# Where the sums of the modulation stand in the expert stages of a diffusion trunk on one core

## The chip, the cores and the metric

One NeuronCore of a Trainium2 chip runs the kernel. The metric is the device time of one execution in microseconds, as the median of several runs. The engines are TensorE (PE: matrix products, with its weight loads shown apart as PEld), VectorE (DVE), ScalarE (ACT), GpSimd (POOL) and SyncE (SP), which issues the loads.

## The reference, cut to what matters

One step of a hybrid trunk with four layers, on 128 context tokens and 256 latent tokens at a width of 1024, in float32. A layer has a token mixer (gated MLP, Mamba-2 SSD, HGRN2, gated MLP) and then a grouped top-2 mixture of 16 experts. Both sub-layers are modulated by vectors that come from the conditioning, one set for the context and one for the latent tokens:

```python
def modulation(cond, w_mod, b_mod):
    m = jax.nn.silu(cond) @ w_mod + b_mod          # (1024) @ (1024, 6*1024)
    return jnp.split(m[:, None, :], 6, axis=-1)    # shift, scale, gate, twice
...
gate, up = jnp.split(jnp.einsum('ld,edf->lef', xs, w_gu), 2, axis=-1)
hid = jax.nn.silu(gate) * up * cw[..., None]
return jnp.einsum('lef,efd->ld', hid, w_down)
```

The modulation of a layer needs nothing of the tokens, so it can be computed at any time before its layer.

## The kernel before, in words

Everything runs on one core with the order of each engine's work written out by hand; semaphores tie the engines together. All large weights come in chunks of 1 MB through one ring of eight slots in SBUF, in the fixed order of a plan; the loads are issued by SP (L393), each as soon as the chunk that held its slot before has been used.

**The modulation.** A layer has six groups of 1024 modulation values, and a group has four weight chunks (`MOD_GROUP` is 4). The DVE multiplies the rows of a chunk by the conditioning and adds them up over the chunks in `macc`, 128 partitions by 1024 columns for each of the two sets (L1961, L1964; four instructions a chunk). What is left is a sum over the 128 partitions. That is `mod_sum` on TensorE (L1690): for each of the 16 blocks of 128 columns of `macc`, the block is the stationary operand and one column of ones the moving one, and the product is one column of PSUM bank 7. Each float32 product appears in the trace as two passes, so a group is 32 passes of one column. `mod_take` on the DVE (L1972) then reads the 16 columns, adds the bias and writes `mods`. Only after it may the DVE start the next group's `macc`.

**The expert stage.** `experts(l)` on TensorE routes and gathers the tokens and then runs 24 steps (6 windows of 128 tokens, 4 experts each). Step `s` is `gate_up(s)`: eight products of 128x128 by 128x512 (L1877, two passes each, 16 in all) from weight chunks A and B into PSUM bank `s % 2`. After the sixth product stand the two transpositions of the step before (`hidden_over(s - 1)`, L1867, bank 2). Then comes `down(s - 1)`: four products of 128x512 (L1892, 8 passes) from chunk D. ACT computes the SiLU of the gate half (`sg`, L1518) and copies the transposed hidden values (`hidt`, L1493); the DVE forms `hid` (L2182). In layers 0, 1 and 2, 16 of the 24 steps (0, 1, 3, 4, 6, 7, ... 21, 22) also bring one chunk of the next layer's modulation (four groups), which the DVE adds into `macc` after that step's `hid`. A group is complete after steps 4, 10, 16 and 22. TensorE runs its `mod_sum` one step later, after `down` of that step, all 16 products in a row (L1903). The DVE takes the sums two steps after the group's last chunk, behind `hid`. Layer 3 has no layer behind it and no modulation in its expert stage.

Of the kernel before, what the change touches and what calls it, by code (L numbers as in the profile page):

```python
# [55 lines left out]
MOD_GROUP = MODC // 6  # L56
# [5 lines left out]
STEPS = NW * EG  # L62
# [12 lines left out]
def moe_mods(l):  # L75

    n = MODC - 2 * MOD_GROUP
    return {j * STEPS // n: j for j in range(n)} if l + 1 < DEPTH else {}
# [90 lines left out]
def trunk(nc, A, O):  # L169
# [13 lines left out]
    with ctx:  # L183
# [13 lines left out]
        def fixed(name, shape, dt=F32):  # L197
            t = at(name, shape, dt, place[0])
            place[0] += -(-4 * int(np.prod(shape[1:])) // 32) * 32
            return t  # L200
# [16 lines left out]
        mods = fixed("mods", [P, 2, 48, 2])  # L217
# [1179 lines left out]
        def chunk_in(eng, c):  # L1397
            eng.wait_ge(raw_in[slot_of[c]], 16 * fill_of[c])
# [215 lines left out]
        def _(pe):  # L1614
            release = {}

            def claim(b, name, value):

                if b in release:
                    pe.wait_ge(*release[b])  # L1620
                release[b] = (S[name], value)
# [61 lines left out]
            def mod_sum(group, columns=range(2 * KD)):  # L1683

                if 0 in columns:
                    pe.wait_ge(S["mac_step"], 16 * (group_of_mac(group) + 1))
                    claim(7, "mod_read", group + 1)
                for c in columns:
                    j, v = divmod(c, 2)
                    ins = pe.matmul(ps[:, 7, c:c + 1], macc[:, v, j * P:(j + 1) * P], ones[:, 0:1], start=True, stop=True)  # L1690
                if 2 * KD - 1 in columns:
                    ins.then_inc(S["mod_summed"], 1)
# [104 lines left out]
            def experts(l):  # L1797
                n0, q, mods = STEPS * l, 2 * l + 1, moe_mods(l)
# [57 lines left out]
                def whole(what, s, k):  # L1856
                    c = places[l, what][s]
                    return ring[:, slot_of[c], :].rearrange("p (k n) -> p k n", k=k)

                def hidden_over(s):  # L1860
                    pe.wait_ge(S["hid_ready"], n0 + s + 1)
                    if s == 0:
                        claim(2, "hidt_ready", n0 + STEPS)
                    elif s >= 2:
                        pe.wait_ge(S["hidt_ready"], n0 + s - 1)
                    for i in range(2):
                        ins = pe.transpose(ps[:, 2, (s % 2) * DE + i * P:(s % 2) * DE + (i + 1) * P], hid[:, s % 2, i * P:(i + 1) * P], ident[:, :])  # L1867
                    ins.then_inc(S["hidt_done"], 1)

                def gate_up(s):  # L1870
                    w, e = divmod(s, EG)
                    claim(s % 2, "hid_ready", n0 + s + 1)
                    for k in range(KD):
                        what = "AB"[k // 4]
                        if k % 4 == 0:
                            chunk_in(pe, places[l, what][s])
                        ins = pe.matmul(ps[:, s % 2, :], xg[:, w, k, :], whole(what, s, 4)[:, k % 4, :], start=(k == 0), stop=(k == KD - 1))  # L1877
                        if k % 4 == 3:
                            ins.then_inc(S["moe_used"], 1)
                        if s and k == 5:  # L1880
                            hidden_over(s - 1)

                def down(s):
                    w, e = divmod(s, EG)
                    chunk_in(pe, places[l, "D"][s])
                    pe.wait_ge(S["hidt_ready"], n0 + s + 1)
                    if e == 0:
                        for h in range(2):
                            claim(OUT_BANKS[w % 2][h], "olo_ready", 2 * (NW * l + w) + h + 1)
                    for k in range(2):  # L1890
                        for h in range(2):
                            ins = pe.matmul(ps[:, OUT_BANKS[w % 2][h], :], hidt[:, s % 2, k, :], whole("D", s, 2)[:, k, 512 * h:512 * h + 512],  # L1892
                                            start=(e == 0 and k == 0), stop=(e == EG - 1 and k == 1))
                    ins.then_inc(S["moe_used"], 1)
# [3 lines left out]
                for s in range(STEPS):  # L1898
                    gate_up(s)
                    if s:  # L1900
                        down(s - 1)
                        if s - 1 in mods and mods[s - 1] % MOD_GROUP == MOD_GROUP - 1:
                            mod_sum(6 * (l + 1) + 1 + mods[s - 1] // MOD_GROUP)  # L1903
                hidden_over(STEPS - 1)
                down(STEPS - 1)
# [22 lines left out]
            for l in range(DEPTH):  # L1928
                if l % 3 == 0:
                    gmlp(l)  # L1930
                elif l % 3 == 1:
                    pe_ssd(pe, l, claim, release, full, by_token, out_tiles, product, row_blocks, full_block)
                else:
                    pe_hgrn(pe, l, claim, release, full, by_token, out_tiles, mod_sum, product, row_blocks, full_block)
                variance(2 * l, 6 * l + 6 if l + 1 < DEPTH else None)
                if l + 1 < DEPTH:
                    mod_sum(6 * l + 6, range(6, 2 * KD))
                experts(l)
                variance(2 * l + 1)
# [365 lines left out]
```

## Time and profile before

| | |
|---|---|
| median of 3 runs | 2907.91 us (2905.69, 2907.91, 2911.71) |
| profiled execution: span from the first to the last instruction | 2919.7 us |
| its time beside the span | the profile gives none |
| mean granted TensorE clock over the span | 0.913 |
| TensorE busy | 2612.8 us, 89% |
| VectorE busy | 1430.2 us, 49% |
| GpSimd, ScalarE busy | 797.6 us, 752.2 us |
| DMA | 524.41 MB, mean 180 GB/s |

All times are microseconds unless marked ns. The granted clock is a share of full speed: 1.00 is 2.4 GHz, 0.50 is 1.2 GHz, and a value between them is the mean over a stretch that has both. Matmuls overlap at their ends, so what a pass costs in a stream is read from the starts of neighbouring lines, not from its own duration. The profile is of one execution that is not among the three timed ones.

### The profile page before, as it was taken

To read this page: it belongs to the slowest core of one execution; us is meant where nothing else is said; L and a number is where in the kernel's file an instruction comes from. 1 tells how busy PE (TensorE), PEld (TensorE's weight loads), DVE (VectorE), ACT (ScalarE), POOL (GpSimd) and SP (SyncE) were. 2 spreads that over 40 slices of the span, in tenths; PEclk is the share of its full clock that TensorE was granted. 3 is DMA by queue.
4 is the path that set the end of the run, shared out by engine and by line. 5 is a ranking of instruction groups with operands and counts; after the bars stand their busy time and mean duration, and the time that the engine had idled before them with its cause. 6 is when DMAs were issued, how large, how long until landed. Compare 5 with 4: busy or idle time off the path is not lost.

```text
span 2919.7 us, 30216 instructions
## 1 busy us (share of the span) xinstructions
PE 2612.8 (89%) x11960; PEld 1918.1 (66%) x11960; DVE 1430.2 (49%) x1955; ACT 752.2 (26%) x1263; POOL 797.6 (27%) x429
## 2 busy tenths in 40 slices
PE   5779899998898998899998877789999899989997
PEld 3778864445896787744458866676444699864444
DVE  6456553334645676633336389974333415650013
ACT  1132130002454451300013344432001334230111
POOL 3355400001363344000014478830000247500000
PEclk8789889998699998899999878898999899979999
DMA  7443639893241216388944411054989143528881
GB/s 265 168 124 101 193 143 334 321 360 110 76 137 37 73 58 180 137 326 316 362 162 138 143 48 37 24 183 150 332 324 348 51 135 101 149 99 300 301 297 41
DMA packets 291851, 524.41 MB, mean 180 GB/s; under 512 B 9472, under 2 KB 141056, under 8 KB 291328
## 3 DMA queue, kind: packets, MB, share of 16 engines
q1 hardware_dynamic: 288256, 519.33, 51.4%
q10 hardware_dynamic: 3456, 3.15, 0.3%
q8 instruction: 96, 1.57, 0.2%
q14 instruction: 43, 0.35, 0.0%
HBM read 517.73 MB, written 4.72 MB: 179 GB/s over the span
## 4 chain that ended last, share of the span: by engine, by line
PE 75%; DVE 12%; ACT 4%; DMA 3%; issue 3%; POOL 2%; SPq 0%; ACTq 0%; DVEq 0%
PE ps L1877 23%; PE ps L1892 11%; PE ps L1625 6%; PE ps L1626 6%; PE ps L1627 6%; PE ps L1690 3%; DVE macc L1964 2%; POOL wlo L1557 2%; DVE uw L1318 2%; PE ps L1648 1%; PE ps L1816 1%; PE ps L1650 1%; PE ps L1649 1%; PE ps L1840 1%; PE ps L1841 1%
## 5 line engine op out<-in xcount | busy, mean ns | idle before, releaser
L1557 POOL TENSOR_TENSOR wlo<-ring,whi 128x1024 fp32r<-128x1024 f32 x202 | 533.6, 2657 | 1514.3 <-ACT whi L1424 1514.3
L1877 PE MATMUL ps<-ring,xg 128*128 128x512 f32 x1536 | 708.0, 606 | 0.0
L1877 PEld LDWEIGHTS ps<-ring,xg 128*128 128x128 f32 x1536 | 290.5, 194 | 329.6 <-issue 329.2
L1964 DVE SCALAR_TENSOR_TENSOR macc<-ring,cond_s,macc 128x1024 f32<-128x1024 f32 x322 | 438.9, 1424 | 10.6 <-DMA ring<-w_mod 10.6
L2182 DVE SCALAR_TENSOR_TENSOR hid<-ps,cws,sg 128x256 f32<-128x256 f32 x96 | 46.4, 484 | 674.6 <-ACT sg L1518 674.6
L1892 PE MATMUL ps<-ring,hidt 128*128 128x512 f32 x768 | 349.9, 599 | 2.3 <-ACT hidt L1493 2.3
L1625 PE MATMUL ps<-hh,whi 128*128 128x384 f32 x832 | 303.4, 365 | 27.3 <-POOL wlo L1557 21.0
L1626 PE MATMUL ps<-hl,whi 128*128 128x384 f32 x832 | 291.0, 350 | 0.0
L1627 PE MATMUL ps<-hh,wlo 128*128 128x384 f32 x832 | 290.9, 350 | 0.0
L1424 ACT ACTIVATE whi<-ring 128x1024 fp32r<-128x1024 f32 x202 | 207.2, 1055 | 307.4 <-DMA ring<-gmlp_w_out 115.2
L1892 PEld LDWEIGHTS ps<-ring,hidt 128*128 128x128 f32 x768 | 147.4, 193 | 187.4 <-issue 187.4
L1493 ACT ACTIVATE hidt<-ps 128x256 f32<-128x256 f32 x96 | 37.0, 385 | 753.9 <-PE ps L1867 753.9
L1625 PEld LDWEIGHTS ps<-hh,whi 128*128 128x128 f32 x832 | 166.7, 200 | 34.7 <-POOL wlo L1557 23.1
L1648 PE MATMUL ps<-whi,hh 128*128 128x256 f32 x432 | 132.7, 307 | 50.7 <-POOL wlo L1557 46.8
L1626 PEld LDWEIGHTS ps<-hl,whi 128*128 128x128 f32 x832 | 166.9, 201 | 0.5 <-issue 0.5
L1627 PEld LDWEIGHTS ps<-hh,wlo 128*128 128x128 f32 x832 | 165.9, 199 | 0.0
L1649 PE MATMUL ps<-whi,hl 128*128 128x256 f32 x432 | 130.6, 302 | 0.0
L1650 PE MATMUL ps<-wlo,hh 128*128 128x256 f32 x432 | 130.3, 302 | 0.0
L1648 PEld LDWEIGHTS ps<-whi,hh 128*128 128x128 f32 x432 | 91.9, 213 | 52.3 <-POOL wlo L1557 48.0
L1690 PEld LDWEIGHTS ps<-ones,macc 128*128 128x128 f32 x736 | 100.8, 219 | 11.1 <-issue 8.7
L1625 PE MATMUL ps<-gsh,whi 128*128 128x384 f32 x256 | 91.7, 358 | 17.7 <-POOL wlo L1557 17.1
L1690 PE MATMUL ps<-ones,macc 128*128 128x1 f32 x736 | 98.5, 267 | 1.0 <-DVE macc L1964 1.0
(361 smaller groups left out, 4112.3 us busy)
## 6 DMA issues: line engine op xcount, KB each, us to landing
ring<-moe_w_gu SPq DMA_DIRECT2D x192, 1024.0 KB, 7.5
ring<-w_mod SPq DMA_DIRECT2D x96, 1024.0 KB, 8.2
ring<-moe_w_down SPq DMA_DIRECT2D x96, 1024.0 KB, 5.1
ring<-gmlp_w_in SPq DMA_DIRECT2D x32, 1024.0 KB, 5.7
ring<-ssd_w_in SPq DMA_DIRECT2D x21, 1024.0 KB, 5.3
ring<-hgrn_w_in SPq DMA_DIRECT2D x20, 1024.0 KB, 5.2
ring<-gmlp_w_out SPq DMA_DIRECT2D x16, 1024.0 KB, 5.7
ring<-ssd_w_out SPq DMA_DIRECT2D x8, 1024.0 KB, 6.0
```

The costliest lines, as they stand in the source:

```text
L1424: act.activation(split_sub(whi, s0), raw_sub(s0), ACT.Copy).then_inc(S["hi_ready"], 1)
L1557: pool.tensor_tensor(split_sub(wlo, s0), raw_sub(s0), split_sub(whi, s0).bitcast(F32), ALU.subtract).then_inc(S["lo_ready"], 1)
L1625: pe.matmul(out, lhi, rhi, start=first, stop=False)
L1626: pe.matmul(out, lhi, rlo, start=False, stop=False)
L1627: return pe.matmul(out, llo, rhi, start=False, stop=last)
L1648: pe.matmul(outs[t], hh[:, k, tk], pair(whi, k), start=(k == 0), stop=False)
L1649: pe.matmul(outs[t], hl[:, k, tk], pair(whi, k), start=False, stop=False)
L1650: ins = pe.matmul(outs[t], hh[:, k, tk], pair(wlo, k), start=False, stop=(k == KD - 1))
L1690: ins = pe.matmul(ps[:, 7, c:c + 1], macc[:, v, j * P:(j + 1) * P], ones[:, 0:1], start=True, stop=True)
L1877: ins = pe.matmul(ps[:, s % 2, :], xg[:, w, k, :], whole(what, s, 4)[:, k % 4, :], start=(k == 0), stop=(k == KD - 1))
L1892: ins = pe.matmul(ps[:, OUT_BANKS[w % 2][h], :], hidt[:, s % 2, k, :], whole("D", s, 2)[:, k, 512 * h:512 * h + 512], start=(e == 0 and k ...
L1964: ins = dve.scalar_tensor_tensor(out=macc[:, v, :], in0=w[:, k, :], scalar=by, in1=macc[:, v, :], op0=ALU.mult, op1=ALU.add)
```

## The change

Where a group was complete after step `s - 2`, `gate_up(s)` now issues two of the group's 16 single-column products after each of its own eight products. Where there is no such step, after step 22 (`s` would be 24), the row stays where it was, after `down(22)` in step 23. So in each of the layers 0, 1 and 2 the sums of steps 4, 10 and 16 move from the end of steps 5, 11 and 17 into steps 6, 12 and 18. `mod_sum` itself is as before: its waits stand before the first column, its signal after the last.

```diff
                 def gate_up(s):
                     w, e = divmod(s, EG)
+                    group = 6 * (l + 1) + 1 + mods[s - 2] // MOD_GROUP if s - 2 in mods and mods[s - 2] % MOD_GROUP == MOD_GROUP - 1 else None
                     claim(s % 2, "hid_ready", n0 + s + 1)
                     for k in range(KD):
                         what = "AB"[k // 4]
...
                         ins = pe.matmul(ps[:, s % 2, :], xg[:, w, k, :], whole(what, s, 4)[:, k % 4, :], start=(k == 0), stop=(k == KD - 1))
                         if k % 4 == 3:
                             ins.then_inc(S["moe_used"], 1)
+                        if group is not None:
+                            mod_sum(group, range(2 * k, 2 * k + 2))
                         if s and k == 5:
                             hidden_over(s - 1)
...
                     gate_up(s)
                     if s:
                         down(s - 1)
-                        if s - 1 in mods and mods[s - 1] % MOD_GROUP == MOD_GROUP - 1:
+                        if s == STEPS - 1 and mods.get(s - 1, 0) % MOD_GROUP == MOD_GROUP - 1:
                             mod_sum(6 * (l + 1) + 1 + mods[s - 1] // MOD_GROUP)
```

## Rows read from the trace of the kernel before

**Rows 1.** The page, part 1: busy time, share of the span, instructions.

```profile
PE 2612.8 (89%) x11960; PEld 1918.1 (66%) x11960; DVE 1430.2 (49%) x1955; ACT 752.2 (26%) x1263; POOL 797.6 (27%) x429
```

**Rows 2.** The page, part 4: the chain that ended last, by engine and line.

```profile
PE 75%; DVE 12%; ACT 4%; DMA 3%; issue 3%; POOL 2%; SPq 0%; ACTq 0%; DVEq 0%
PE ps L1877 23%; PE ps L1892 11%; PE ps L1625 6%; PE ps L1626 6%; PE ps L1627 6%; PE ps L1690 3%; DVE macc L1964 2%; POOL wlo L1557 2%; DVE uw L1318 2%; PE ps L1648 1%; PE ps L1816 1%; PE ps L1650 1%; PE ps L1649 1%; PE ps L1840 1%; PE ps L1841 1%
```

**Rows 3.** Windows, expert stages 0 and 3: engines' busy time, PEclk, DMA share, GB/s.

```profile
416.00:692.00 276.00, 275.43 (x754) 131.54 (x755) 93.45 (x110) 23.93 (x58) 0.00 (x0) 0.97 0.86 316
...
2621.00:2875.00 254.00, 253.44 (x630) 114.16 (x629) 20.79 (x42) 23.98 (x59) 0.00 (x0) 1.00 0.78 265
```

**Rows 4.** TensorE's waits, 416 to 692 us: total, times, longest.

```profile
PE ps L1892 <- ACT hidt L1493: 0.6, 1, 0.6
```

**Rows 5.** TensorE's timeline, expert stage of layer 0: start, duration, line, count.

```profile
455.01 5.31 PE L1877 MATMUL ps<-ring,xg 128*128 128x512 f32 x12
460.16 0.38 PE L1867 MATMUL ps<-ident,hid 128*128 128x128 f32 x2
460.37 1.88 PE L1877 MATMUL ps<-ring,xg 128*128 128x512 f32 x4
...
476.05 4.29 PE L1690 MATMUL ps<-ones,macc 128*128 128x1 f32 x32
480.20 8.10 PE L1877 MATMUL ps<-ring,xg 128*128 128x512 f32 x12
488.13 0.38 PE L1867 MATMUL ps<-ident,hid 128*128 128x128 f32 x2
...
490.07 3.60 PE L1892 MATMUL ps<-ring,hidt 128*128 128x512 f32 x8
...
546.11 3.63 PE L1690 MATMUL ps<-ones,macc 128*128 128x1 f32 x32
549.60 7.09 PE L1877 MATMUL ps<-ring,xg 128*128 128x512 f32 x12
...
556.53 0.38 PE L1867 MATMUL ps<-ident,hid 128*128 128x128 f32 x2
```

**Rows 6.** Windows of 12 us from the start of sums 1, 2, 3, layer 0.

```profile
476.00:488.00 12.00, 12.00 (x45) 7.50 (x44) 0.00 (x0) 0.00 (x0) 0.00 (x0) 0.72 1.02 379
546.00:558.00 12.00, 12.00 (x50) 7.19 (x49) 0.00 (x0) 0.39 (x1) 0.00 (x0) 0.86 0.83 314
614.00:626.00 12.00, 12.00 (x50) 7.17 (x49) 0.00 (x0) 0.39 (x1) 0.00 (x0) 0.86 1.00 387
```

**Rows 7.** Timeline of the weight loads around the first sum.

```profile
475.62 0.19 PEld L1690 LDWEIGHTS ps<-ones,macc 128*128 128x128 f32 x1 [0.24 <-issue]
476.05 4.20 PEld L1690 LDWEIGHTS ps<-ones,macc 128*128 128x128 f32 x31 [0.24 <-issue]
```

**Rows 8.** Windows of the SSD and the HGRN stage with short products.

```profile
885.00:905.00 20.00, 15.20 (x111) 11.91 (x112) 16.18 (x19) 9.49 (x10) 8.71 (x3) 1.00 0.07 27
1859.00:1880.00 21.00, 15.00 (x135) 13.12 (x133) 20.81 (x29) 10.40 (x20) 20.22 (x17) 1.00 0.06 21
```

**Rows 9.** The DVE's timeline around the first sum of layer 0.

```profile
467.56 4.86 DVE L1964 SCALAR_TENSOR_TENSOR macc<-ring,cond_s,macc 128x1024 f32<-128x1024 f32 x4
473.23 0.48 DVE L2182 SCALAR_TENSOR_TENSOR hid<-ps,cws,sg 128x256 f32<-128x256 f32 x1 [0.81 <-ACT sg L1518]
490.69 0.48 DVE L2182 SCALAR_TENSOR_TENSOR hid<-ps,cws,sg 128x256 f32<-128x256 f32 x1 [16.97 <-ACT sg L1518]
491.09 0.17 DVE L1972 TENSOR_TENSOR mods<-ps,cols 128x16 f32<-128x16 f32 x1
```

**Rows 10.** What SP's load queue waited for, 440 to 680 us.

```profile
SPq L393 <- PE ps L1877: 98.5, 32, 10.0
SPq L393 <- DVE macc L1964: 84.1, 14, 9.8
SPq L393 <- PE ps L1892: 18.2, 7, 3.0
```

## The prediction

> **What bounds the kernel now.** I read the page first. TensorE is busy for 89% of the span and the chain that ended last runs through it for 75%; the gate and up products (L1877) alone are 23% of that chain and the down products (L1892) 11% [rows 1, 2]. So the expert stages are TensorE's own, and whatever lengthens TensorE's stream in them lengthens the kernel. To be sure of it I asked what TensorE waited for inside the expert stage of layer 0: one wait of 0.6 us in 276 us [rows 4]; layers 1 and 2 answer with the same line. Then I compared stages: layer 0's expert stage, which carries 16 chunks of the next layer's modulation, lasts 276 us at a granted clock of 0.97, and layer 3's, which carries none, lasts 254 us at 1.00 [rows 3]. The 22 us between them are what the modulation costs TensorE. No product of the modulation runs there except the four sums (L1690), so the 22 us are the sums and what they do to their neighbours.
>
> The timeline of TensorE shows both. A step without a sum is regular: 12 passes of L1877 from 455.01 to 460.16 (5.15 us, 0.429 us a pass; each product is two passes), two transpositions, 4 more passes, 8 passes of the down product [rows 5]. The sum of 16 single-column products is 32 passes: 546.11 to 549.60, 3.49 us, 0.109 us a pass. The 12 gate passes behind it need 6.93 us (549.60 to 556.53) instead of 5.15. Behind the first sum of the layer it is worse: from the start of the sum to the transpositions 12.08 us (476.05 to 488.13), where 3.49 + 5.15 = 8.64 would do; behind the second it is 10.42 us. The losses are 3.44 and 1.78 us.
>
> The windows say where they come from: in the 12 us from the start of a sum the granted clock is 0.72 at the first sum of a layer (three rows) and 0.86 at the others (nine) [rows 6]. The clock has two levels, 2.4 and 1.2 GHz, so a mean of 0.72 over 12 us costs 0.28 x 12 = 3.36 us and one of 0.86 costs 1.68 us, which is the loss just read from the timeline. Layers 1 and 2 repeat layer 0, 0.72 and then three times 0.86. What TensorE did before each fall was the same all twelve times: dense 512-column passes at 1.00, and then 3.5 us of single-column passes. Check: four sums of 3.49 us and 3.36 + 3 x 1.68 us of lost clock are 22.4 us, against 22 between the stages.
>
> **The change, part by part.** *What moves.* Three sums of four in each of layers 0, 1 and 2 (those behind steps 4, 10 and 16) go from a row at the end of steps 5, 11 and 17 into the gate products of steps 6, 12 and 18: two sums (four passes) behind each of the eight products. The fourth sum of each layer is after step 22, keeps its row and its loss. Nine sums change; no instruction is added or taken away, and no DMA is moved.
>
> *The passes themselves: no change.* At 0.109 us a single-column pass costs its weight load. In a row the first load runs while the last down pass still streams (load at 475.62, down pass to 476.05), and the other 31 follow one another [rows 7]; with the load for the next gate pass 32 loads lie open. In pairs, the first load of each four lies beside a 0.429 us gate pass, three more and the one for the returning gate pass lie open: 8 x 4 = 32 again. So 8 x 4 x 0.109 = 3.49 us either way. That switching costs nothing extra is seen at the transpositions, which already stand between gate products: 460.16 to 460.37 for two, and the gate passes before and behind keep 0.43 us [rows 5]. The trace has no switch to a single column and back inside a product, so bounds: nothing from below (the count of open loads cannot go under 32), and from above one more open load of 0.109 us at each of eight returns, 0.87 us a sum, 7.8 us for nine. I take nothing, as the transpositions are the nearest row.
>
> *The clock: the gain.* In the new place TensorE does 0.86 us of 512-column passes, then 0.44 us of single-column ones, and so on: two thirds of each round are dense. Nearest rows: stretches of 20 us in the SSD and HGRN stages with a TensorE that is busy for 15.2 of 20 and for 15.0 of 21 us, in short products with waits between, keep a granted 1.00 [rows 8]; the row that loses the clock has no dense pass for 3.5 us. I therefore take it that the clock stays at its full level through the nine products. Then the nine losses go: as profiled 3 x (3.36 + 1.68 + 1.68) = 20.2 us by the windows, 21.0 us by the timeline; if only the smaller loss is counted nine times, 9 x 1.68 to 9 x 1.78, 15 to 16 us.
>
> *Waits.* The wait for the accumulation (macc, L1964) now stands behind the first gate product instead of behind the down product; behind it on TensorE's queue are the other seven gate products. The DVE finished that macc at 472.42, 3.6 us before the sum began at 476.05 [rows 5, 9], and the new place is 0.86 us later: no wait. The signal to the DVE comes with the last pair, 0.44 us after the last gate pass. The DVE wants it only after the step's hid: the gate passes ended at about 490.07, and it took the sums at 491.09 [rows 5, 9], so 0.6 us are to spare; if they were not, the DVE, idle for 17 us ahead of that hid, would start one accumulation some tenths later. The transpositions of step 6 wait for hid of step 5, done at 473.71 [rows 9]. The first four gate products release their slot after 8 passes and three pairs of sums instead of after the row and 8 passes, the last four 0.44 us before the last pair ends: no slot of the ring is released later in the stream than now.
>
> *Weights.* A faster TensorE asks for its weights sooner. The loads' queue waited 98.5 + 84.1 + 18.2 us in the 240 us from 440 to 680 for slots to be released, not for transfers [rows 10]; the stage moves 316 GB/s [rows 3], 6.7 us less makes that 324, and 387 GB/s stand in a 12 us window of it [rows 6]. I take nothing; the bound is the whole gain.
>
> *Sum.* Between -20 or -21 us (the profiled losses) and -15 (all nine the smaller). The page gives a span of 2919.7 us and no other time of that execution; the timed median is 2907.91, 11.8 us less. So the profiled execution is a slow one of its kind, and where its sums fell 0.72 others may have paid 0.86. I take -16 us, near the smaller loss, on the median: 2907.9 - 16 = 2892 us.
>
> **The rivals.** *The switches cost (B).* The clock stays, but each return opens a load: 7.8 us of the 16 are eaten, 2900 us. For it: no row shows this very switch; against it: the transpositions.
>
> *The clock falls inside the product (C, slower).* A third of each round is still single-column, and if that is enough, the half level comes in the middle of the gate product and meets more work than now. Were the whole product at half clock (16 passes of 0.429 and 32 of 0.109 us), it would lose 6.9 + 3.5 = 10.4 us, against 16/9 = 1.8 us now: +8.6 us, nine times +77 us, 2985 us. With half of the product at half clock it is 5.2 us, +3.4 each, 2939 us. It decides against the change once a product loses more than 1.8 us. Against it stand the stretches of rows 8; for it, that none of them has this mix. The Trainium skill ("TensorE: Matmul & The Clock Gate", section "A second HAM failure mode: psum-queue depth-cycling") tells of a kernel that cycles through PSUM banks each iteration and idles so often between groups that the clock swings between its levels; by that rule the eight trips from the gate bank to the sums' bank would bring rival C. The trace does not bear it out so far: a step goes through gate, transposition and output banks at 1.00 [rows 5, 3].
>
> *The time is given back (D, no change).* The earlier TensorE meets late weights: the stage's DMA share is 0.86 and 1.00 or more in some windows [rows 3, 6]. Then PE would wait for the ring what it gained, 2908 us. Against it, that the loads wait for slots; and that TensorE has no such wait now.
>
> **How the numbers follow.** Forecast (A): 0.80; B 0.08, C 0.06, D 0.06. Measured medians of this kernel spread by 6 us over three runs, so 0.2% (5.8 us) is about what can be told from no change. A alone: from 21 us (all losses of the profile) to 11 us, if the three rows that stay find the larger loss instead of the smaller (3 x 1.68 = 5 us less than 16): 2887 to 2897. With some scatter below, and B above, the range is 2884 to 2901. Faster is A and B, 0.88; same D, 0.06; slower C, 0.06.
>
> **What would show it.** Right: in the timeline of steps 6, 12 and 18 the passes alternate, 2 of L1877 and 4 of L1690, some 1.3 us a round; the granted clock of these products is 1.00; the three stages are some 269 to 271 us at 0.99; the fourth sum still has 0.86 or 0.72 behind it. Wrong: a clock under 1 in those products (C), rounds of 1.4 us (B), a wait of TensorE for the ring (D), or a wait of the DVE for the sums in the middle of the stage.

## The result and the profile after

The changed kernel takes 2894.82 us in the median of six runs, the kernel before 2909.81 us in the same rounds. The ratio is 0.9934, with a 95% interval of 0.9917 to 0.9951, which is 14 to 24 us less. A second set of rounds gave 2890.94 against 2910.88 us, 0.9924 (0.9908 to 0.9941). The forecast was 2892 us, 16 us less.

The windows of 12 us from the start of the sums, after (columns as in [rows 3]), and the three expert stages from their first to their last product:

```profile
470.00:482.00 12.00, 12.00 (x54) 7.36 (x53) 1.11 (x3) 0.77 (x2) 0.00 (x0) 1.00 1.01 390
537.00:549.00 12.00, 12.00 (x54) 7.36 (x53) 0.48 (x1) 0.77 (x2) 0.00 (x0) 1.00 0.94 347
604.00:616.00 12.00, 12.00 (x54) 7.38 (x54) 1.81 (x5) 0.77 (x2) 0.00 (x0) 1.00 1.02 390
670.00:682.00 12.00, 11.16 (x55) 7.81 (x54) 1.82 (x4) 2.66 (x5) 0.16 (x1) 0.86 0.00 0
...
410.60:679.10 268.50, 267.94 (x753) 128.35 (x751) 93.22 (x109) 23.82 (x58) 0.00 (x0) 0.99 0.88 325
1213.10:1483.10 270.00, 269.44 (x753) 128.78 (x752) 93.27 (x109) 23.82 (x58) 0.00 (x0) 0.99 0.87 323
1984.60:2254.60 270.00, 269.44 (x753) 128.79 (x752) 93.24 (x109) 23.82 (x58) 0.00 (x0) 0.99 0.87 323
```

The clock column is the one to read: 1.00 at the three moved sums, where [rows 6] has 0.72, 0.86 and 0.86, and 0.86 behind the fourth sum, which kept its row. The other two layers have 1.00 at their three moved sums as well. The same three stages before, between the same two points:

```profile
416.58:691.98 275.40, 274.83 (x753) 131.21 (x752) 93.25 (x109) 23.93 (x58) 0.00 (x0) 0.97 0.86 317
1229.14:1504.44 275.30, 274.73 (x753) 131.26 (x751) 93.26 (x109) 23.92 (x58) 0.00 (x0) 0.97 0.86 317
2007.48:2282.73 275.25, 274.69 (x753) 131.28 (x752) 93.22 (x109) 23.92 (x58) 0.00 (x0) 0.97 0.86 317
```

Together they are 17.5 us shorter after the change.

The timeline of TensorE in step 6 of layer 0 and the weight loads at its start, after:

```profile
470.10 1.02 PE L1878 MATMUL ps<-ring,xg 128*128 128x512 f32 x2
470.96 0.50 PE L1690 MATMUL ps<-ones,macc 128*128 128x1 f32 x4
471.32 1.10 PE L1878 MATMUL ps<-ring,xg 128*128 128x512 f32 x2
472.27 0.50 PE L1690 MATMUL ps<-ones,macc 128*128 128x1 f32 x4
472.63 1.10 PE L1878 MATMUL ps<-ring,xg 128*128 128x512 f32 x2
...
480.27 0.50 PE L1690 MATMUL ps<-ones,macc 128*128 128x1 f32 x4
480.63 3.68 PE L1895 MATMUL ps<-ring,hidt 128*128 128x512 f32 x8
```

```profile
470.53 0.19 PEld L1690 LDWEIGHTS ps<-ones,macc 128*128 128x128 f32 x1 [0.24 <-issue]
470.96 0.41 PEld L1690 LDWEIGHTS ps<-ones,macc 128*128 128x128 f32 x3 [0.24 <-issue]
471.30 0.30 PEld L1878 LDWEIGHTS ps<-ring,xg 128*128 128x128 f32 x2
```

Two gate passes, four single-column passes, and the next round 1.31 us after the last (471.32 to 472.63). The whole product runs from 470.10 to 480.63, 10.53 us, with its two transpositions; the same passes summed at the prices of [rows 5] are 16 x 0.429 + 32 x 0.109 + 0.21 = 10.56 us. So in this product the passes cost neither less nor more than in a row. The first load of each four lies beside a gate pass (470.53), the other three follow.

The waits: TensorE's in the stage, the DVE's for the sums, and those of the load queue from 440 to 680 us, after:

```profile
PE ps L1895 <- ACT hidt L1493: 0.6, 1, 0.6
```

```profile
DVE mods L1975 <- PE ps L1690: 6.0, 1, 6.0
```

```profile
SPq L393 <- PE ps L1878: 88.1, 31, 5.0
SPq L393 <- DVE macc L1967: 84.4, 14, 9.8
SPq L393 <- PE ps L1895: 15.2, 6, 3.0
```

In the stage TensorE waits where it did in [rows 4] and for nothing else. The DVE has one wait for the sums in the stage, that of the fourth group, whose row did not move; it was 6.0 us before as well. The load queue still waits for slots, 188 of 240 us instead of 201 in [rows 10]: the weights are a little less ahead and not late.

The spans of the two profiles are 33.8 us apart, 2919.7 and 2885.9. Only 17.5 of that lie in the stages. The rest lies where no instruction differs, and it is not counted as gain: the first gate pass of layer 0, for one, starts at 410.63 instead of 416.58. How far such parts differ by themselves is seen below at one kernel profiled twice.

### The profile page after: what moved, and what is told of

It is laid out like the page before. It is cut to its first block, busy times and chain, and to the rows that moved or that the text cites. A ratio compares the mean times of both kernels' runs of the same rounds, so it can differ in the third digit from the quotient of the medians.

```text
span 2885.9 us, 30216 instructions
## 1 busy us (share of the span) xinstructions
PE 2576.5 (89%) x11960; PEld 1897.3 (66%) x11960; DVE 1437.3 (50%) x1955; ACT 751.0 (26%) x1263; POOL 797.0 (28%) x429
## 4 chain that ended last, share of the span: by engine, by line
PE 73%; DVE 13%; ACT 4%; DMA 3%; issue 3%; POOL 2%; SPq 0%; ACTq 0%; DVEq 0%
PE ps L1878 23%; PE ps L1895 12%; PE ps L1625 6%; PE ps L1626 6%; PE ps L1627 6%; DVE macc L1967 3%; PE ps L1690 2%; POOL wlo L1557 2%; DVE uw L1318 2%; PE ps L1648 1%; PE ps L1816 1%; PE ps L1650 1%; PE ps L1649 1%; PE ps L1840 1%; PE ps L1841 1%
## 5 line engine op out<-in xcount | busy, mean ns | idle before, releaser
L1878 PEld LDWEIGHTS ps<-ring,xg 128*128 128x128 f32 x1536 | 280.5, 190 | 296.7 <-issue 296.3
```

## The experiments

Theory: a row of single-column passes is followed by a fall of TensorE's clock to its lower level, and the change gives back what the passes behind it lost. Rivals: the later place, with its waits and signals, makes the gain; the passes are hidden better in pairs; or switching costs something and the gain is what is left.

**The later place, but a row.** The 16 sums stand behind the first gate product of the later step.

```diff
-                        if group is not None:
-                            mod_sum(group, range(2 * k, 2 * k + 2))
+                        if group is not None and k == 0:
+                            mod_sum(group)
```

> All 16 sums of the nine groups stand as one row behind the first gate product of the later step: the place and the waits of the change, without the pairs. Theory (the gain is the granted clock, which falls behind a row of 3.5 us with no dense pass): the clock falls as before, 0.86 or 0.72 in the 12 us from the start of each row, the expert stages of layers 0 to 2 last 273 to 277 us again, and the time is that of the kernel before, within 5 us. Rival (the gain comes of the later place, its waits or its signals): stages of 268 to 270 us and 15 to 20 us less than before.

Measured: 0.9993 of the kernel before (0.998 to 1.0006), 2908.42 us; the stages are 273.8, 273.9 and 273.9 us. The place without the pairs brings nothing that can be told from zero. One thing was not expected. Its timeline in layer 1, first and second sum, and the windows from the start of the first, second and third:

```profile
1282.28 3.63 PE L1690 MATMUL ps<-ones,macc 128*128 128x1 f32 x32
1285.77 4.54 PE L1878 MATMUL ps<-ring,xg 128*128 128x512 f32 x10
```

```profile
1348.98 3.91 PE L1690 MATMUL ps<-ones,macc 128*128 128x1 f32 x32
1352.75 5.94 PE L1878 MATMUL ps<-ring,xg 128*128 128x512 f32 x10
```

```profile
1282.00:1294.00 12.00, 12.00 (x55) 7.40 (x54) 1.29 (x4) 0.77 (x2) 0.00 (x0) 1.00 1.01 390
1349.00:1361.00 12.00, 12.00 (x51) 7.53 (x50) 0.00 (x0) 0.72 (x2) 0.00 (x0) 0.86 0.84 299
1417.00:1429.00 12.00, 12.00 (x47) 7.42 (x46) 0.00 (x0) 0.00 (x0) 0.00 (x0) 0.72 0.96 367
```

The same row, between the same neighbours, once loses nothing, once 1.7 and once 3.4 us. In layer 2 the first row loses nothing either. So a row is no fixed price: of the nine moved rows in this profile two lose nothing, five 1.7 and two 3.4 us, 15.3 us in all. In the profile before, all twelve rows happened to lose. What decides it for a single row was not tried.

**Two half rows.** 8 sums behind the fourth and 8 behind the eighth gate product.

```diff
-                            mod_sum(group, range(2 * k, 2 * k + 2))
+                        if group is not None and k % 4 == 3:
+                            mod_sum(group, range(2 * (k - 3), 2 * (k - 3) + 8))
```

> The 16 sums stand in two half rows, 8 behind the fourth and 8 behind the eighth gate product (1.75 us each). Theory in its wide form (what counts is that dense passes stand near enough on both sides): the clock stays at 1.00, stages of 268 to 270 us, the time of the changed kernel within 5 us. Theory in its narrow form (only a fine mix keeps the clock): granted 0.86 behind some half rows, and between 0 and 15 us less than before. Rival (the passes themselves are hidden better in pairs): some 7 us slower than the changed kernel at a clock of 1.00.

Measured: 0.9940 (0.9921 to 0.9958), 2893.63 us, as the changed kernel. A half row in its timeline, and the window behind the first product:

```profile
478.29 1.84 PE L1690 MATMUL ps<-ones,macc 128*128 128x1 f32 x16
479.99 1.96 PE L1878 MATMUL ps<-ring,xg 128*128 128x512 f32 x4
```

```profile
478.00:490.00 12.00, 12.00 (x55) 7.41 (x54) 4.37 (x6) 0.77 (x2) 0.00 (x0) 1.00 1.04 401
```

None of the 18 half rows of 1.7 us is followed by a fall. The pairs are not needed, and the finer mix of the changed kernel hides nothing more that can be told from the noise.

**Four behind each down product, all twelve groups.** The sums stay in the step where the row stood. The chunk's slot is still released by the last down product, ahead of the last four sums.

```diff
+                    group = 6 * (l + 1) + 1 + mods[s] // MOD_GROUP if s in mods and mods[s] % MOD_GROUP == MOD_GROUP - 1 else None
...
-                    ins.then_inc(S["moe_used"], 1)
+                            if k == 1 and h == 1:
+                                ins.then_inc(S["moe_used"], 1)
+                            if group is not None:
+                                mod_sum(group, range(8 * k + 4 * h, 8 * k + 4 * h + 4))
...
-                        if s - 1 in mods and mods[s - 1] % MOD_GROUP == MOD_GROUP - 1:
-                            mod_sum(6 * (l + 1) + 1 + mods[s - 1] // MOD_GROUP)
```

> As before the sums follow the group's last chunk by one step, but four of them stand behind each of the four down products, for all four groups of a layer. Half of each round (0.86 us dense, 0.87 us single-column) is dense. Theory: the place does not matter, the clock stays at 1.00 for all twelve groups; the three stages are 266 to 268 us, the twelve losses of 1.7 to 3.4 us go, and the time is 2 to 8 us under the changed kernel. Rival (something of the gate products or of the step of delay makes the gain): the time of before, within 5 us. Rival (a half is not dense enough): the clock falls in the down products, slower than before.

Measured: 0.9913 (0.9898 to 0.9928), 2885.92 us. It was run once more beside the changed kernel, in the same rounds:

> The changed kernel as it is, on the chip and in the rounds of the four-in-down kernel, so that the two can be set side by side. Theory: 14 to 20 us less than before, stages of layers 0 to 2 of 268 to 271 us, each with the loss behind the fourth row alone.

> Four sums behind each down product, all twelve groups, once more. Theory: no fall of the clock in the expert stages, 267.1 us each, and the three fourth rows' losses (1.3 to 2.9 us a layer) less than the changed kernel: 4 to 9 us under it. Rival: the same time as the changed kernel, if the end of the stage hides the fourth row's loss.

Measured: changed kernel 2890.94 us, 0.9924 (0.9908 to 0.9941); four in down 2886.06 us, 0.9912 (0.9896 to 0.9928). Over both sets, 12 runs of each, the means are 2892.8 and 2886.3 us, 6.4 us apart with a 95% interval of 2.6 to 10.3. The start of the rounds in its first profile, and the three stages in its second:

```profile
470.19 1.02 PE L1893 MATMUL ps<-ring,hidt 128*128 128x512 f32 x2
471.04 0.95 PE L1690 MATMUL ps<-ones,macc 128*128 128x1 f32 x8
471.85 1.10 PE L1893 MATMUL ps<-ring,hidt 128*128 128x512 f32 x2
```

```profile
415.50:682.80 267.30, 266.74 (x754) 127.80 (x753) 93.23 (x109) 23.82 (x58) 0.00 (x0) 1.00 0.88 326
1212.70:1479.80 267.10, 266.54 (x753) 127.69 (x751) 93.28 (x109) 23.82 (x58) 0.00 (x0) 1.00 0.88 326
1982.60:2249.70 267.10, 266.54 (x752) 127.71 (x752) 93.23 (x109) 23.82 (x58) 0.00 (x0) 1.00 0.88 326
```

All three stages hold 1.00, where the changed kernel's have 0.99 for the fourth row (268.5, 270.0 and 270.0 us, and 268.6, 270.0 and 268.5 us in its second profile). So neither the gate products nor the step of delay make the gain, the fourth row's loss is real time, and this version beats both kernels. In its two profiles the six stages are 267.1 us each, and still the spans are 2891.6 and 2879.8 us: 11.8 us come and go outside these stages. The mean granted clock over the span is 0.923 and 0.927, which is 223 and 210 us of lost clock (span times what is missing to 1): the difference is of the size of the missing time.

**Only 2 of the 16 products,** in the row of the kernel before and in the pairs of the changed one. 14 columns of the modulation are left out in the nine groups.

```diff
-                            mod_sum(6 * (l + 1) + 1 + mods[s - 1] // MOD_GROUP)
+                            mod_sum(6 * (l + 1) + 1 + mods[s - 1] // MOD_GROUP, (0, 15) if s < STEPS - 1 else range(16))
```

```diff
-                        if group is not None:
-                            mod_sum(group, range(2 * k, 2 * k + 2))
+                        if group is not None and k in (0, KD - 1):
+                            mod_sum(group, (0,) if k == 0 else (15,))
```

> The kernel before, but in the nine rows only the first and the last of the 16 products are issued (the other 14 columns of the modulation are left out): 4 passes in place of 32. Theory (a row costs 3.49 us of passes and 1.7 to 3.4 us of lost clock): the clock stays at 1.00 behind them, each row gives back 28 x 0.109 = 3.05 us and its loss, in all 9 x 3.05 + 15 to 20 = 42 to 48 us less than before. Rival (the loss is not the row's, but a wait or a switch at that place): 27 us less than before, and a clock of 0.86 still behind the four passes.

> The changed kernel, but of the 16 products only the first (behind the first gate product) and the last (behind the eighth) are issued; 14 columns of the modulation are left out. Theory: nothing but the 28 passes a group is saved, 9 x 3.05 = 27 us less than the changed kernel, some 43 us less than before, and the same time as the row with 2 of 16, within 5 us: with the passes gone the two places are equal. Rival (the pairs hide part of their passes): less than 27 us under the changed kernel. Rival (switching costs something at each return): more than 27 us, up to 33.

Measured: 0.9835 (0.9815 to 0.9854), 2865.60 us, and 0.9845 (0.9827 to 0.9864), 2866.37 us, beside 2910.29 us. The first is 48 us less than before by its ratio and 45 by the medians, the second 45 and 44, so with most of the passes gone the two places cannot be told apart. The row of 4 passes, what follows it, and the window:

```profile
474.87 0.50 PE L1690 MATMUL ps<-ones,macc 128*128 128x1 f32 x4
475.23 5.40 PE L1877 MATMUL ps<-ring,xg 128*128 128x512 f32 x12
480.46 0.38 PE L1867 MATMUL ps<-ident,hid 128*128 128x128 f32 x2
```

```profile
470.00:482.00 12.00, 12.00 (x34) 5.59 (x33) 1.73 (x3) 1.07 (x3) 0.00 (x0) 1.00 0.77 291
```

Twelve gate passes in 5.23 us (475.23 to 480.46) and no fall. Of the 45 to 48 us, 9 x 3.05 = 27 are passes; 17 to 20 are left for the clock. From the changed kernel only the passes are left to take: 2892.8 - 2868.2 us in the means, which are of different rounds, 25 us, against 27 expected.

**A row of 12, and the same row eight times over.** Once 12 sums behind the fourth and 4 behind the eighth gate product; once the changed kernel with each pair issued six times, 12 products behind every gate product.

```diff
-                            mod_sum(group, range(2 * k, 2 * k + 2))
+                        if group is not None and k % 4 == 3:
+                            mod_sum(group, range(0, 12) if k == 3 else range(12, 16))
```

```diff
-                            mod_sum(group, range(2 * k, 2 * k + 2))
+                            mod_sum(group, 6 * [2 * k, 2 * k + 1])
```

> As the two half rows, but 12 sums behind the fourth gate product and 4 behind the eighth: the longer stretch has 2.6 us of single-column passes, between dense passes of 3.4 us on both sides. Theory in which the length of the row decides by itself: the clock falls behind most of the nine. Theory in which dense work near enough on both sides keeps it: it falls behind some or none, 8 to 20 us less than before.

> The changed kernel with each pair of sums issued six times over (the same columns again, 12 products, 2.6 us, behind each of the eight gate products): single-column stretches as long as those of the row of 12, but with only 0.86 us of dense passes between them, a quarter of each round. The passes alone add 9 x 8 x 20 x 0.109 = 157 us to the changed kernel, about 3051 us. Theory in which the share of dense work decides: the clock falls in these products and stays low for most of each, up to 24 us lost in each product, 100 to 220 us more again. Theory in which only the length of a stretch counts: the clock does as in the row of 12.

Measured: the row of 12 takes 2910.43 us, 0.9996 (0.9984 to 1.0009): the whole gain is gone. The first product in its timeline, and the windows from the start of the first two and the fourth row of layer 0 and of the first row of layer 1:

```profile
479.12 2.73 PE L1690 MATMUL ps<-ones,macc 128*128 128x1 f32 x24
481.71 3.61 PE L1878 MATMUL ps<-ring,xg 128*128 128x512 f32 x4
```

```profile
479.00:491.00 12.00, 12.00 (x50) 7.13 (x49) 3.23 (x6) 0.77 (x2) 0.00 (x0) 0.86 1.04 401
547.00:559.00 12.00, 12.00 (x50) 7.15 (x49) 0.48 (x1) 0.77 (x2) 0.00 (x0) 0.86 0.79 295
...
681.00:693.00 12.00, 11.44 (x50) 8.05 (x49) 0.51 (x2) 1.35 (x3) 0.00 (x0) 0.72 0.00 0
...
1288.00:1300.00 12.00, 12.00 (x54) 7.38 (x54) 4.28 (x6) 0.77 (x2) 0.00 (x0) 1.00 1.04 401
```

Eight of its nine rows of 2.6 us are followed by 0.86, one by 1.00: 8 x 1.7 = 13.6 us, little less than the 15.3 us of the nine whole rows at the later place. The fourth rows, which stand as before, happen to lose 3.4 us each in this profile (0.72 in all three layers) and 1.7 in that of the whole rows, so the equal times do not show that the two kinds of row lose exactly the same. The theory that dense work near enough on both sides keeps the clock left 8 to 20 us of gain, and it was wrong: a row three quarters as long brings nearly the whole loss.

Twelve in each pair takes 3268.87 us, 1.1222 (1.12 to 1.1244), 358 us more than before, where I had set 240 to 360 (157 of passes and 100 to 220 of clock, less the change's 16). Its timeline in layer 0 and the window from 484 to 528 us:

```profile
474.54 1.02 PE L1878 MATMUL ps<-ring,xg 128*128 128x512 f32 x2
475.40 2.73 PE L1690 MATMUL ps<-ones,macc 128*128 128x1 f32 x24
478.00 1.10 PE L1878 MATMUL ps<-ring,xg 128*128 128x512 f32 x2
478.94 3.48 PE L1690 MATMUL ps<-ones,macc 128*128 128x1 f32 x24
482.29 2.05 PE L1878 MATMUL ps<-ring,xg 128*128 128x512 f32 x2
484.13 5.12 PE L1690 MATMUL ps<-ones,macc 128*128 128x1 f32 x24
```

```profile
484.00:528.00 44.00, 44.00 (x163) 36.12 (x162) 4.37 (x6) 0.77 (x2) 0.00 (x0) 0.50 0.19 67
```

The clock falls at the second stretch and then stays at 0.50. This is the prediction's rival C made to happen: with stretches as long as in the row of 12, but eight of them with only two gate passes between, each product loses not 1.7 but some 25 us (stages of 394.7 us; less 267.1 and the 3 x 17.4 us of added passes, 75 us in three products). The number of stretches and the dense work between them were changed together, so which of the two does it is not shown.

## Why the prediction was right

**TensorE is the bound, and nothing takes the gain back.** Right. The waits of the stage are those of before, and the load queue still waits for slots. Rival D did not come, and TensorE has no wait for the ring.

**The passes cost the same in pairs.** Right: 10.53 us against 10.56 for a product. The upper bound, one more open load at each return (rival B), is excluded by the rounds of 1.31 us, where it would make 1.40, and the kernels with 2 of 16 agree: 25 us for 27 expected, where switching that costs something would have shown more than 27.

**The clock stays up.** Right in all nine products, and the row at the later place shows that it is this and not the place. The prediction's reason was a choice of nearest rows, [rows 8], which have another mix; only the runs show that the clock holds, with four passes behind a product as here, with eight, and with half rows of 16. One reading behind it is not exact: before each fall it sees 3.5 us of single-column passes. The first row of layer 0 takes 4.15 us instead of 3.49 (476.05 to 480.20 in [rows 5]), and from 476.1 to 480.2 the granted clock is 0.83, so there the fall came before the row had ended. The trace of before could thus have told that less than a whole row can be enough, as the row of 12 then showed.

The rival of bank trips (C) did not come: the passes go back and forth between the gate's and the sums' bank at a granted 1.00, and TensorE is busy for 10.50 of the 10.50 us from 470.1 to 480.6. The Trainium skill ("TensorE: Matmul & The Clock Gate", section "A second HAM failure mode: psum-queue depth-cycling") tells of a kernel that idles between its groups, and these products do not. The experiment with twelve in each pair shows that the clock can fall inside a product, so C was a fair rival and only its condition was not met. What it is in a row that brings the clock down, its single columns, its weight loads or its missing dense passes, was not tried apart.

**The size, 16 us.** Right within what could be measured, at its low end: the first rounds give 14 to 24 us, the second 17 to 27. The term to look at is the loss of a row. I took nearly the smaller loss for all nine. A stage without a fall lasts 267.1 us; with four rows it lasted 275.3 us in the profile before and 273.8 us with the row at the later place, so four rows cost 8.2 and 6.7 us, although single ones lose nothing; three of four in three stages are 9/4 of that, 15 to 18 us. In the two profiles themselves the moved rows had 20.2 us by the windows and the stages got 17.5 us shorter. The fourth rows took the rest: after the change the stages of layers 1 and 2 are 270.0 us, 2.9 us over 267.1, where the fourth rows of before had 0.86 and 1.7 us each. The prediction had counted that as a possibility and left it out of the sum. It differs from one execution to the next: in the second profile of the changed kernel only layer 1 has it (270.0 us).

**The profiled execution of before.** That its span was 11.8 us over the median was used as a reason to take less. It is no good reason: the kernel with two profiles shows that as much can come from other stages. So the mechanism was right, and that 16 us was taken rather than the profiled 20 rests in part on a reason that does not hold; the medians, 15 and 20 us less, do not tell the two apart. Why the clock falls more often in one execution than in another was not tried.

## What to carry to other kernels

A run of single-column products that is bound by its weight loads looks busy in the profile, but the dense passes behind it may pay for it at the lower clock; compare the granted clock before and behind it, not the busy share. Where there are independent dense products, put a few of the small ones behind each of them: the number of passes stays, the place hardly matters, and halves of a row did as well as pairs here, while three quarters in one piece lost the whole gain. The small ones must stay few: twelve behind each product took 358 us more than before, 157 of them added passes. Fix every such row, also the last one: the version with all twelve beats the one with nine. TensorE runs 736 of these passes in this kernel and only 384 of them in the expert stages; a row of 32 outside, at 2561.70 us of the profile before, takes 4.25 us, with a granted clock of 0.81 from there to 2566.0. What a mix would give there was not tried.

## What the runs showed of the hardware that was not expected

- A row of 32 single-column passes (3.5 us) between the same dense neighbours was followed by a loss of 0, 1.7 or 3.4 us in one and the same execution.
- 24 passes in a row (2.6 us) were followed by a loss of 1.7 us in eight of nine places, and the kernel was as slow as with 32 (0.9996 against 0.9993 of the time before); 16 (1.7 us) lost nothing in any of 18 places.
- One kernel, profiled twice, had spans of 2891.6 and 2879.8 us, at mean granted clocks of 0.923 and 0.927, with its three expert stages of 267.1 us equal.
